# S1 to S4 of an FFN's token blocks from accumulated turns on TensorE, and one tile difference on GpSimd

## What is computed

```
x = LN(ALPHA*x + 0.5*((silu(x@w1) * (x@w3)) @ w2))      # FFN, D_FF = 2816
x = LN(ALPHA*x + mixer(x))                               # layer 0: pooling, layer 1: stick-breaking attention
x = LN(ALPHA*x + 0.5*((silu(x@w1) * (x@w3)) @ w2))       # second FFN
x = LN(ALPHA*x + sigmoid(x@w_gate + b_gate) * (p@w_proj))# per-layer input embedding
```

## Time and profile before

| | before |
|---|---|
| median of 3 runs | 2495.22 us |
| lowest, highest | 2495.19, 2495.64 us |
| profiled execution | 2500.3 us |
| its span, first to last instruction | 2498.6 us |
| mean granted TensorE clock | 0.99 of full |
| TensorE busy | 2427.4 us, 97% |
| VectorE busy | 1660.6 us, 66% |
| ScalarE busy | 1102.9 us, 44% |
| GpSimd busy | 470.5 us, 19% |

### The profile page before, as it was taken

How to read it: one execution, slowest core, us unless ns; L and a number is a source line. 1 busy time by engine, 2 the same in 40 slices (tenths; PEclk the granted TensorE clock), 3 DMA queues, 4 the chain that set the end, 5 groups by cost and what they waited for, 6 DMA issues and landing times.

```text
span 2498.6 us, 38673 instructions
## 1 busy us (share of the span) xinstructions
PE 2427.4 (97%) x15358; PEld 2174.5 (87%) x15358; DVE 1660.6 (66%) x2166; ACT 1102.9 (44%) x1769; POOL 470.5 (19%) x399
## 2 busy tenths in 40 slices
PE   7999999989999999899999999999999999999998
PEld 7999999879999998799999988777776799999986
DVE  5866666877666676776666662666666776666667
ACT  4433343344333343543344333666665443344343
POOL 4211123222211110311121101122123321111100
PEclk9999999999999999999999999999999999999999
DMA  4322222223222223132222225777876132322231
GB/s 132 94 79 85 85 85 93 60 73 98 75 85 85 85 94 94 41 95 85 85 85 85 84 77 148 207 194 206 230 203 182 45 109 80 95 85 73 82 102 68
DMA packets 376642, 259.14 MB, mean 104 GB/s; under 512 B 10321, under 2 KB 339025, under 8 KB 376464
## 3 DMA queue, kind: packets, MB, share of 16 engines
q1 hardware_dynamic: 371360, 239.64, 33.3%
q0 software_dynamic: 5104, 17.04, 2.1%
HBM read 248.22 MB, written 8.42 MB: 103 GB/s over the span
## 4 chain that ended last, share of the span: by engine, by line
PE 86%; DVE 7%; ACT 3%; issue 3%; DMA 1%; POOL 0%; SPq 0%; DVEq 0%; ACTq 0%
PE ps L2496 77%; PE ps L797 5%; PE ps L829 2%; DVE ring L1884 1%; DVE x L1956 1%; DVE x L1942 1%; DVE small L1902 1%; PE ps L905 0%; ACT ring L1373 0%; DMA raw<-in_ffn_w_dram 0%; PE ps L2545 0%; PE ps L2602 0%; ACT e_buf L1582 0%; ACT xt_hi L1391 0%; POOL t_buf L1151 0%
## 5 line engine op out<-in xcount | busy, mean ns | idle before, releaser
L2496 PE MATMUL ps<-xt_hi,ring 128*128 128x320 f32 (+2 forms) x3328 | 791.2, 313 | 22.3 <-DVE tmp L2052 8.7
L2496 PEld LDWEIGHTS ps<-xt_hi,ring 128*128 128x128 f32 x3328 | 576.7, 191 | 35.1 <-DVE tmp L2052 9.6
L2496 PE MATMUL ps<-ring,h_hi 128*128 128x512 f32 x1760 | 556.7, 392 | 8.5 <-DVE x L1942 4.6
L1884 DVE TENSOR_TENSOR ring<-raw,ring 128x1024 fp32r<-128x1024 f32 (+1 forms) x318 | 437.2, 1378 | 129.3 <-ACT ring L1373 129.1
L2496 PE MATMUL ps<-xt_lo,ring 128*128 128x320 f32 (+2 forms) x1664 | 518.8, 312 | 0.0
L2496 PE MATMUL ps<-s_ops,ring 128*128 128x320 f32 x3168 | 510.5, 311 | 7.7 <-DVE s_ops L2015 7.7
L2496 PEld LDWEIGHTS ps<-s_ops,ring 128*128 128x128 f32 x3168 | 479.5, 189 | 8.7 <-DVE s_ops L2015 8.7
L2496 PEld LDWEIGHTS ps<-ring,h_hi 128*128 128x128 f32 x1760 | 331.5, 188 | 82.8 <-DVE x L1942 6.3
L1373 ACT ACTIVATE ring<-raw 128x1024 fp32r<-128x1024 f32 (+1 forms) x318 | 287.3, 931 | 238.0 <-PE ps L2496 211.8
L1151 POOL TENSOR_TENSOR t_buf<-raw,t_buf 128x512 f32<-128x512 f32 x88 | 115.9, 1317 | 1346.0 <-DVE t_buf L1897 1346.0
L2496 PE MATMUL ps<-ring,h_lo 128*128 128x512 f32 x880 | 344.0, 391 | 0.0
(11 more groups left out here) (188 smaller groups left out, 2505.4 us busy)
## 6 DMA issues: line engine op xcount, KB each, us to landing
raw<-in_ffn_w_dram SPq DMA_DIRECT2D x264, 512.0 KB, 4.1
k_raw<-in_cache_k_dram SPq DMA_DIRECT2D x128, 256.0 KB, 5.0
v_raw<-in_cache_v_dram SPq DMA_DIRECT2D x128, 256.0 KB, 4.3
raw<-in_sb_w_in_dram SPq DMA_DIRECT2D x24, 512.0 KB, 5.5
raw<-in_ple_w_gate_dram SPq DMA_DIRECT2D x16, 512.0 KB, 3.9
g_b<-in_ln_g_dram POOLq DMA_DIRECT2D x8, 512.0 KB, 5.6
b_b<-in_ln_b_dram POOLq DMA_DIRECT2D x8, 512.0 KB, 7.1
raw<-in_sb_w_out_dram SPq DMA_DIRECT2D x8, 512.0 KB, 5.8
```

The source lines that it names most:

```text
L1884: ve.tensor_tensor(ring[:, slot, 1, col:col + cols], conversion_source(u), ring[:, slot, 0, col:col + cols].bitcast(F32), ALU.subtract).th ...
L2496: return pe.matmul(out, w, xx, start=first, stop=last, skip_group_check=True)
```

## The change

S1 and S2 of a pair are no longer formed ahead: TensorE turns the left and the right half of the tile of x onto the same PSUM columns, the second added to the first, once for S1 and once for S2; from S2's bank it subtracts the high and low halves of x11, which lie in SBUF (16 turns and two matmuls of 512 columns instead of 8 turns). For S3 and S4 only the difference of two whole tiles is made, `pair_diff`: S3 is the turned left half (4 turns), S4 the turned left and right halves added (8 turns). Pair 0's difference is made by VectorE (`left_diffs`), pair 1's by VectorE in the first FFN and by GpSimd behind its quarter sums in the others. `pair_sums`, `pair_sums12` and `pair_sums43` go.

With it the order is changed by hand in several places. S43a is turned directly behind S12a and changes banks with S12b. The low half of S12a is made by TensorE (`subtract_sums12`) and ScalarE (`low_sums12` on ScalarE) at three entries; the low halves of x's pieces in the embed stage go from ScalarE to VectorE. C(0) follows B(0) in the order of items. S43b comes ahead of p6(0), p2(2) ahead of p5(0) in the first FFN too. VectorE's first_diffs(1) stands behind low_sums43 of pair 1; gate_of_first(0) goes into the stage before; in the pool stage spread(2) and normalise(2) go ahead of first_diffs and mix(3). In the embed stage all three turns lie within the last two gate products; the subtraction of the previous stage's x2 comes two chunks later.

```diff
@@ -126,7 +126,7 @@
-BLOCK_PIECES = (("x0", 4), ("x1", 6), ("x2", 4), ("S12a", 6), ("S12b", 4), ("S43a", 6), ("S43b", 6), ("X22", 6))
+BLOCK_PIECES = (("x0", 4), ("x1", 6), ("x2", 4), ("S12a", 6), ("S43a", 4), ("S12b", 6), ("S43b", 6), ("X22", 6))
@@ -215,7 +215,7 @@
-            by_act = st.kind != "load" and name[0] == "x"
+            by_act = st.kind in ("ffn", "pool", "out") and name[0] == "x" or st.kind != "load" and name == "S12a"
@@ -262,12 +262,14 @@
-            if st.prev.kind != "load":
+            if st.prev.kind == "load":
+                up(0)
+                first_diffs(0)
...
-            up(0)
-            first_diffs(0)
-            if st.prev.kind == "load":
+            else:
...
+                first_diffs(0)
+                up(0)
@@ -1170,22 +1164,9 @@
-            def pair_sums(st):
-                f = st.next.f
-                if st.kind == "load":
-                    pool.wait_ge(x_loaded[0], 16)
-                    pool.wait_ge(x_loaded[2], 16)
-                else:
-                    pool.wait_ge(x_norm, st.norm0 + ORDER.index(2) + 1)
-                pool.wait_ge(quarter_lo, 3 * f + 3)
-                pool.tensor_tensor(sums_block(0), x[:, 2, 0:HK], x[:, 2, HK:], ALU.add).then_inc(sums_a, 1)
-                pool.wait_ge(sums_a, 4 * f + 1)
-                pool.tensor_tensor(sums_block(1), sums_block(0), x[:, 0, 0:HK], ALU.subtract).then_inc(sums_a, 1)
-                pool.tensor_tensor(sums_block(3), x[:, 0, 0:HK], x[:, 2, 0:HK], ALU.subtract).then_inc(sums_a, 1)
-                pool.wait_ge(sums_a, 4 * f + 2)
-                pool.tensor_tensor(sums_block(2), x[:, 0, HK:], sums_block(1), ALU.subtract).then_inc(sums_a, 1)
+                if st.kind != "load":
+                    pool.wait_ge(x_norm, st.norm0 + TILES)
+                    pool.tensor_tensor(pair_diff[:, 1, :], x[:, 1, :], x[:, 3, :], ALU.subtract).then_inc(diff_b, 1)
@@ -1493,16 +1480,24 @@
                 unit = st.item
-                if prev.kind != "load":
+                if prev.kind == "load":
+                    first_product(st, 0)
+                    cvt_to(unit["B", 0] + 1)
+                    first_product(st, 1)
+                    silu_of_first(st, 0)
+                    hi_sums12(prev, 0)
+                    hi_sums43(prev, 0)
+                    hi_sums12(prev, 1)
+                    cvt_to(unit["A", 2] + 1)
+                else:
                     se.preload_act_table(ACT.Silu)
-                first_product(st, 0)
-                cvt_to(unit["B", 0] + 1)
-                first_product(st, 1)
-                silu_of_first(st, 0)
-                hi_sums12(prev, 0)
-                hi_sums12(prev, 1)
-                cvt_to(unit["A", 2] + 1)
-                hi_sums43(prev, 0)
+                    hi_sums12(prev, 0)
+                    first_product(st, 1)
+                    low_sums12(prev, 0)
+                    hi_sums43(prev, 0)
+                    hi_sums12(prev, 1)
+                    cvt_to(unit["C", 0] + 1)
+                    silu_of_first(st, 0)
                 first_product(st, 2)
@@ -1776,8 +1771,9 @@
-                    cvt_to(unit["C", 0] + 1)
...
+                    cvt_to(unit["B", 0] + 1)
+                    first_product(st.next, 0)
@@ -1805,17 +1801,17 @@
                             hi(st, t - 2)
+                        if t == 3:
+                            hi(st, 2)
+                        if t == 4 and st.then == "blocks":
+                            first_product(st.next, 0)
                         deviation(st, t)
-                        if t in (2, 3):
-                            low(st, t - 2)
                         if t < TILES - 1:
...
                         if t == 3 and st.then == "blocks":
+                            cvt_to(st.next.item["A", 2] + 1)
                             quarter_rounded(st)
-                            hi(st, 2)
-                            cvt_to(st.next.item["A", 2] + 1)
-                            low(st, 2)
-                            cvt_to(st.next.item["C", 0] + 1)
+                            cvt_to(st.next.item["B", 0] + 1)
                 if st.kind == "pool":
@@ -2023,24 +2021,20 @@
-            def pair_sums12(st):
-                f = st.next.f
+            def left_diffs(st):
...
-                    ve.wait_ge(x_loaded[1], 16)
-                    ve.wait_ge(x_loaded[3], 16)
+                    ve.wait_ge(x_loaded[0], 16)
+                    ve.wait_ge(x_loaded[2], 16)
...
-                    ve.wait_ge(x_norm, st.norm0 + TILES)
-                ve.tensor_tensor(sums_right[:, 0, :], x[:, 3, 0:HK], x[:, 3, HK:], ALU.add).then_inc(sums_b, 1)
-                ve.wait_ge(sums_b, 4 * f + 1)
-                ve.tensor_tensor(sums_right[:, 1, :], sums_right[:, 0, :], x[:, 1, 0:HK], ALU.subtract).then_inc(sums_b, 1)
-            def pair_sums43(st):
-                f = st.next.f
-                ve.tensor_tensor(sums_right[:, 3, :], x[:, 1, 0:HK], x[:, 3, 0:HK], ALU.subtract).then_inc(sums_b, 1)
-                ve.wait_ge(sums_b, 4 * f + 2)
-                ve.tensor_tensor(sums_right[:, 2, :], x[:, 1, HK:], sums_right[:, 1, :], ALU.subtract).then_inc(sums_b, 1)
+                    ve.wait_ge(x_norm, st.norm0 + ORDER.index(2) + 1)
+                ve.tensor_tensor(pair_diff[:, 0, :], x[:, 0, :], x[:, 2, :], ALU.subtract).then_inc(diff_a, 1)
+            def right_diffs(st):
+                ve.wait_ge(x_loaded[1], 16)
+                ve.wait_ge(x_loaded[3], 16)
+                ve.tensor_tensor(pair_diff[:, 1, :], x[:, 1, :], x[:, 3, :], ALU.subtract).then_inc(diff_b, 1)
@@ -2094,25 +2088,26 @@
                 if prev.kind == "load":
-                    pair_sums12(prev)
-                    pair_sums43(prev)
+                    left_diffs(prev)
+                    right_diffs(prev)
                     gate_of_first(st, 0)
+                    low_sums12(prev, 0)
+                    cvt_to(unit["B", 0] + 1)
+                    low_sums43(prev, 0)
+                    gate_of_first(st, 1)
+                    low_sums12(prev, 1)
+                    cvt_to(unit["A", 2] + 1)
                 else:
-                    gate_of_first(st, 0)
-                    pair_sums12(prev)
-                low_sums12(prev, 0)
-                cvt_to(unit["B", 0] + 1)
-                low_sums12(prev, 1)
-                gate_of_first(st, 1)
-                cvt_to(unit["A", 2] + 1)
-                if prev.kind != "load":
-                    pair_sums43(prev)
-                low_sums43(prev, 0)
+                    cvt_to(unit["B", 0] + 1)
+                    gate_of_first(st, 1)
+                    cvt_to(unit["C", 0] + 1)
+                    low_sums43(prev, 0)
+                    low_sums12(prev, 1)
                 cvt_to(unit["D", 0] + 1)
+                low_sums43(prev, 1)
                 first_diffs(st, 1)
-                low_sums43(prev, 1)
+                hidden_of_first(st, 0)
                 cvt_to(unit["B", 1] + 1)
-                hidden_of_first(st, 0)
                 up_of_second(st, 0)
@@ -2380,13 +2375,16 @@
                         evacuate(st, TILES + j)
-                        normalise(st, j)
-                        if 1 <= j <= 3:
-                            low(st, j - 1)
+                        if j == TILES - 1:
+                            centre(st, j)
+                            gate_of_first(st.next, 0)
+                            rescale(st, j)
+                        else:
+                            normalise(st, j)
                         if j == 2:
...
                         if j == 3:
-                            cvt_to(unit["C", 0] + 1)
+                            left_diffs(st)
                 if st.kind == "embed":
@@ -2467,11 +2470,11 @@
                     low(prev, 4)
+                    spread(2)
+                    normalise(st, 2)
                     first_diffs(st.next, 0)
...
                     low(st, 0)
-                    spread(2)
-                    normalise(st, 2)
                     low(st, 1)
@@ -2479,8 +2482,11 @@
                     normalise(st, 3)
+                    left_diffs(st)
                     spread(4)
-                    normalise(st, 4)
+                    centre(st, 4)
+                    gate_of_first(st.next, 0)
+                    rescale(st, 4)
                 if st.kind == "v":
@@ -2594,25 +2600,42 @@
-            def turn_block(st, name, first, second):
-                bank = piece_banks(st, name)
-                for n, block in enumerate((first, second)):
-                    for c in range(HC):
-                        ins = pe.transpose(ps[:, bank + n, c * P:(c + 1) * P], block[:, c * P:(c + 1) * P], ident)
+            def turn_sum(bank, first, second):
+                for block in (first, second):
+                    for c in range(HC if block is not None else 0):
```

(52 more changed lines are left out.)

47 lines of the change are left out of this document (25 added, 22 removed).

## The result

The changed kernel takes **2519.2 us** (median of 4 executions, 2517.6 to 2520.1); it is slower than the kernel before by a ratio of 1.0091, 95% interval 1.0073 to 1.0108. A second set of executions, on another chip, gave 2519.2 us again and 1.0084 (1.0067 to 1.0101). The prediction, 2504.7 us and 2492 to 2512, had the sign right and the size wrong: the time lies 7 us above the upper end of its range.

A forecast was written before the change was run, and what follows sets the result against it. TensorE, busy 97%, was taken as the bound, with its waits and half-clock stretches. Load +2.4, pool +7.6, embed -1.9, out +3.1 and starts -1.7 sum to +9.5 on 2495.2: 2504.7 us, range 2492 to 2512.

The forecast's parts named there:

- Pool order: Pool into second FFN: first_diffs(0) behind normalise(2) delays GpSimd's sums and ScalarE's rounding, p1(0) +6.9 us; whole entry +7.6.
- Rival (a): Pool stage: the new order costs nothing, 6.9 and 2.5 us go, 2495 us in all; chance 0.2.
- The slow start behind the wait: Pool into second FFN: TensorE, idle 8 us before p1(0), starts at the half clock, +2.5 us.
- The wait before p5(0): FFN entry: ScalarE's and VectorE's in-order chain through C(0) to pair 1's low half makes TensorE wait 3.3 us.
- Rival (b): FFN entries: VectorE keeps up at p5(0), so wait and slow stretch go at three entries, 2487 us; chance 0.12.
- Its slow stretch: FFN entry, behind the 3.3 us wait before p5(0): TensorE runs at 1.2 GHz for a while, costing 2.5 us.
- The load behind first_diffs(1): FFN entry: moved first_diffs(1) releases the third up weights' buffer late; DMA lands 4.1 us later, first_diffs(2) +3.1 us.
- Turns: FFN entries: t12 2.05 us against 0.79, t43 +0.40; with S12a's subtraction 14.6 us more on TensorE in all.
- Rival (d): TensorE at FFN entries: each turn accumulating onto PSUM takes twice as long, 2527 us; chance 0.03.
- Rival (c): FFN entries: 28 turns in a row let the clock fall, p2(1) and t12(1) run slow, 2511 us; chance 0.1.
- Embed: Embed into third FFN: copy waits and three subtractions go, VectorE's third low half ends 1.1 us late; -1.9 us.
- Starts of embed and v: Embed and v starts: later subtraction of x2 loses three waits for ScalarE, 0.76 and two of about 0.45; -1.7 us.

The follow-up runs named there:

- e1: Changed kernel with the pool stage's VectorE order undone (first_diffs and mix(3) again ahead of spread(2) and normalise(2)): 2509.1 us, ratio to before 1.0043.
- e7: Kernel before with only the pool stage's VectorE move (spread(2) and normalise(2) ahead of first_diffs and mix(3)): 2506.1 us, ratio 1.0032.
- e3: Changed kernel with ScalarE converting C(0) ahead of its rounding of pair 1's S1 and S2 instead of behind it: 2507.6 us, ratio to before 1.0036.
- e8: Changed kernel with GpSimd's gain and bias loads moved behind the differences of the fourth quarter of gate weights: 2507.9 us, ratio to before 1.0040.
- e2: Changed kernel with VectorE's first_diffs(1) again ahead of the low half of S4 and S3 of pair 1: 2505.9 us, ratio to before 1.0032.
- e10: Changed kernel with pool order restored, C(0) and first_diffs(1) earlier, and A(2) converted and split earlier in the first FFN: 2480.3 us, ratio to before 0.9934.
- e6: Kernel before with only VectorE's first_diffs(1) moved behind the low half of S4 and S3 of pair 1: 2507.4 us, ratio 1.0042.

## Why the prediction was right in sign and wrong in size

**Pool order: right.** first_diffs(0) was laid out for 7.2 us after the stage's first turn and came 7.1 after; p1(0) +6.9, measured +7.3. Rival (a) falls by e1 and e7: 10.1 us less and 7.2 us more. The slow start behind the wait was priced at 2.5: p1(0) to X22 came out at 32.8 us against 33.8 forecast, so it was priced 1 us too high. (The steps behind the last sum add up to 509.6 and not to the 509.8 that stands there; nothing hangs on it.)

**The wait before p5(0): right in place, cause and length** (3.3 forecast, 2.99 three times; e3). Rival (b), that it wouldn't be there, falls. Its slow stretch was priced too high: 2.5 forecast, 1.3 to 1.6 by the stretch p5(0) to X22 against e3's. In the embed entry the sum had charged another 1.6 us for a second slow stretch, which didn't come: p1(0) to X22 took 31.1 us, 32.9 forecast.

**The load behind first_diffs(1): the step that failed.** The step read "Its DMA lands 4.1 us later (median)". The chain was right, and its last link, the transfer, was priced by the median of 264 transfers, though the kernel before makes this very one at 1996.1 us and its row says 6.4. It took 6.3 to 6.8 us in the changed kernel, and the stretch from X22 to p5(2) is 2.4 to 2.6 us longer than forecast at each of four entries: 9.9 us in the traces, more than the 7.7 by which the sum of +9.5 fell short of the traced +17.2. Slow stretches that were priced too high (above: 2.5 us each where 1.3 to 1.6 came, 1.6 where none came) hid a part of it. The range had for it only "the load bound or not", which reaches down and not up. That is the mis-sized term. e8 takes it away alone (10.2 us in the four stretches, 11.2 in the median), e2 together with the 1.0 us of lateness (14.3 and 13.3).

**Turns: nearly right.** 16 turns take 1.66 us, 0.104 each, 12 take 1.34; a t12 is 2.21 and a t43 1.34 ahead of a subtraction and 1.23 ahead of a product, where 2.05 and 1.19 stood: some 0.5 us an entry too little. Rival (d) falls:

```profile
1993.85 1.91 PE L2551 MATMUL ps<-ident_r,x 128*128 128x128 f32 x16
1995.51 0.48 PE L2502 MATMUL ps<-xt_hi,neg_ident 128*128 128x512 f32 x1
...
1996.06 1.47 PE L2551 MATMUL ps<-ident_r,pair_diff 128*128 128x128 f32 x12
1997.40 0.50 PE L2502 MATMUL ps<-xt_hi,neg_ident 128*128 128x512 f32 x1
```

**Rival (c), the clock behind 28 turns: falls.** The stretch of the turns and the product p2(1) behind them ran at the full clock in the out entry (rows below). At the three other entries the product behind the turns took 1.75 to 1.84 us, which is the full clock too.

```profile
1993.80:1997.40 3.60, 3.60 (x32) 3.35 (x31) 1.56 (x2) 1.14 (x3) 3.09 (x1) 1.00 0.00 0
1997.90:1999.70 1.80, 1.80 (x13) 1.76 (x13) 0.00 (x0) 1.54 (x3) 0.00 (x0) 1.00 0.00 0
```

The Trainium skill says in "TensorE: Matmul & The Clock Gate", Part 4 (PE-mode transpose), that transposes don't count as activity in the way that matmuls do. No sign of it is seen in this kernel, whose turns are issued with is_transpose (L2551): the clock held over 28 of them and two subtractions in 3.6 us. Whether it would hold over a longer row of turns no run shows.

**Embed: right on its main step** (p1(0) 5.0 us sooner, 4.8 forecast; it waits 1.28 us for VectorE's third low half, 1.1 forecast).

**Starts of embed and v: wrong.** The subtraction that moved is x2's, which had no wait. The three waits that were to go belong to x3's, and are all there: of the 11.5 us on ScalarE's high half, 8.1 and 1.3 are the pool's, and the other three times 0.5, 0.8 and 0.8. No gain instead of 1.7. The reading of the waits had a slip of its own, without effect on the sum: the four on the sum of gate products don't lie one at each entry, but two in the pool's, one in embed's and one in out's.

**The base.** Putting differences between traces on a median of three executions lost 3.7 us (2495.2 against 2498.9), which the 46 executions show and three could not.

## What to carry to other kernels

Price a transfer on a chain by its own row in the trace, not by the median of its line: one that is early hides what it shares its engines with. When an instruction is moved back on an engine, follow what its result releases, down to the buffer and the load; three places in this kernel's order cost 35 us and hid a gain of 14.5. On an in-order engine, put a conversion whose data are there ahead of one that must wait for TensorE: at the four entries here that took 2 us of a wait away each time and delayed nothing that TensorE waited for (e3, e10).

## What the runs showed of the hardware

- The third up weights, a load of 512 KB, took 3.7 to 4.0 us from issue to landing where no gain or bias load was beside them (e8, four entries). With two 512 KB loads of gain and bias issued by GpSimd within 0.6 us of them, they took 6.2 to 6.8 us, in e1 also 7.4 and 8.5.
- A wait of TensorE is followed by a stretch at 1.2 GHz in some executions and not in others: behind 2.91 us the clock stayed at 1.00 in e7 and was 0.67 over ten microseconds in the kernel before; behind 1.88 us (on the sum of gate products, fourth FFN) three products took 6.9 us in two traces of the kernel before and 5.4 in e6. Behind waits of 1.75 (e6) and 1.61 us (e10) they took 5.4 as well. Behind the 2.99 us before p5(0) there was a slow stretch in thirteen entries of fifteen. So the same wait has no single price, and the first entry took 70.2 and 71.6 us in two traces of the changed kernel.
- Turns of 128 x 128 at the full clock: sixteen, of which eight add onto PSUM, take 0.104 us each; twelve, of which four do, 0.102 to 0.112; eight that don't, 0.099.
